# Second network of a two-block transformer: high weights meet high and low tokens in one product of 512 columns, and VectorE adds the halves of the bank

## The reference, cut to what matters

```
D_MODEL = 1024; SEQ = 256; D_FF = 4 * D_MODEL
def squared_relu_mlp(h, w1, w2):
    return jnp.square(jax.nn.relu(h @ w1)) @ w2
...
    h = modulate(rms_norm(x, norm_g[i, 2]), sh2, sc2)
    x = x + gt2 * rms_norm(squared_relu_mlp(h, mlp_w1[i], mlp_w2[i]), norm_g[i, 3])
```

## Time and profile before

| | |
|---|---|
| median of three runs | 2341.97 us (2341.75 to 2345.68) |
| the profiled execution, its own time | 2343.54 us |
| its span in the trace | 2341.7 us |
| mean granted TensorE clock | 0.975 of full speed |
| TensorE matmul / VectorE / ScalarE busy | 95% / 62% / 41% |
| `mlp_up` in the trace | from 1311.0 to 1408.4 us |
| `mlp_down` in the trace | from 1408.4 to 1505.7 us |

### The profile page before, as it was taken

One profiled execution on the slowest core, in us unless ns is written; L12 is line 12 of the kernel. 1 busy time (PEld: TensorE's weight loads), 2 busy tenths in 40 slices (PEclk: granted clock), 3 DMA queues, 4 the chain that ended last, 5 costly groups with the idle time before them and its releaser, 6 DMA issues.

```text
span 2341.7 us, 48560 instructions
## 1 busy us (share of the span) xinstructions
PE 2233.3 (95%) x21500; PEld 1848.0 (79%) x21500; DVE 1453.8 (62%) x2539; ACT 970.8 (41%) x1716; POOL 85.2 (4%) x83
## 2 busy tenths in 40 slices
PE   8999999999999999999999999998999999899998
PEld 5864488888867789999997899895677879677786
DVE  3274436867657356887763556665475877656577
ACT  2244333322323223443332563344355655544565
POOL 1000000000010000000000001020000002000000
PEclk8999999999999999999999999999999999999999
DMA  8335238656522100000002347554365853204485
GB/s 356 108 105 220 90 126 305 245 211 229 220 110 90 54 1 3 4 4 4 13 3 112 141 174 263 196 180 173 134 219 211 335 215 134 73 1 180 169 340 192
DMA packets 47745, 348.11 MB, mean 149 GB/s; under 512 B 5312, under 2 KB 5328, under 8 KB 6320
## 3 DMA queue, kind: packets, MB, share of 16 engines
q1 hardware_dynamic: 46368, 334.52, 38.2%
q0 software_dynamic: 1168, 10.50, 1.1%
HBM read 343.95 MB, written 1.05 MB: 147 GB/s over the span
## 4 chain that ended last, share of the span: by engine, by line
PE 52%; DVE 8%; ACT 3%; issue 1%; DVEq 0%; ACTq 0%
PE banks L549 10%; PE banks L2245 6%; PE banks L2257 5%; PE banks L1037 4%; PE banks L3179 3%; PE banks L3180 3%; PE banks L3181 3%; PE banks L3210 2%; PE banks L3212 2%; PE banks L3211 2%; PE banks L561 1%; PE banks L2097 1%; PE banks L2304 1%; PE banks L2279 1%; PE banks L3228 1%
## 5 line engine op out<-in xcount | busy, mean ns | idle before, releaser
L527 DVE TENSOR_TENSOR moe_w_low<-weight_slots,moe_w_high 128x2048 fp32r<-128x2048 f32 x96 | 217.9, 2288 | 61.7 <-ACT moe_w_high L518 61.0
L527 DVE TENSOR_TENSOR mlp_w_low<-weight_slots,mlp_w_high 128x2048 fp32r<-128x2048 f32 x64 | 146.5, 2288 | 157.3 <-ACT mlp_w_high L518 157.3
L518 ACT ACTIVATE mlp_w_high<-weight_slots 128x2048 fp32r<-128x2048 f32 x64 | 122.3, 1910 | 178.7 <-PE banks L549 118.9
L518 ACT ACTIVATE moe_w_high<-weight_slots 128x2048 fp32r<-128x2048 f32 x96 | 181.7, 1914 | 23.5 <-PE banks L3212 19.8
L1037 PE MATMUL banks<-arena,weight_slots 128*128 128x256 f32 (+1 forms) x512 | 141.5, 438 | 2.9 <-DVE arena L2846 1.5
L1037 PEld LDWEIGHTS banks<-arena,weight_slots 128*128 128x128 f32 x512 | 98.4, 193 | 44.3 <-issue 33.9
L3179 PE MATMUL banks<-moe_w_high,slots_x 128*128 128x512 f32 x320 | 130.3, 407 | 2.8 <-DVE moe_w_low L527 2.8
L3180 PE MATMUL banks<-moe_w_low,slots_x 128*128 128x512 f32 x320 | 126.9, 397 | 0.0
L3181 PE MATMUL banks<-moe_w_high,slots_x 128*128 128x512 f32 x320 | 126.8, 396 | 0.0
L686 DVE SCALAR_TENSOR_TENSOR arena<-weight_slots,silu_c,arena 128x256 f32<-128x256 f32 x288 | 119.0, 481 | 0.0
L2245 PE MATMUL banks<-arena 64*64 64x64 f32 (+1 forms) x1600 | 81.2, 233 | 0.0
(11 more groups left out here) (454 smaller groups left out, 5239.9 us busy)
## 6 DMA issues: line engine op xcount, KB each, us to landing
weight_slots<-weights SPq DMA_DIRECT2D x318, 1024.0 KB, 4.9
arena<-small POOLq DMA_DIRECT2D x1, 2560.0 KB, 8.9
arena<-x_t POOLq DMA_DIRECT2D x1, 2048.0 KB, 12.5
arena<-bias POOLq DMA_DIRECT2D x1, 2048.0 KB, 12.6
constants<-consts POOLq DMA_DIRECT2D x1, 1395.0 KB, 17.9
out_t<-arena SPq DMA_DIRECT2D x4, 256.0 KB, 2.3
parameters<-params POOLq DMA_DIRECT2D x1, 763.0 KB, 21.8
arena<-pool_inv POOLq DMA_DIRECT2D x1, 512.0 KB, 14.9
```

The source lines that it names most:

```text
L518: nc.scalar.activation(self.pair(j)[0], slot(j, 0, SLOT), ACT.Copy).then_inc(*act.step("high", j))
L527: nc.vector.tensor_tensor(self.pair(j)[1], slot(j, 0, SLOT), self.pair(j)[0], ALU.subtract).then_inc(*v.step("used", j))
```

## The change

In `mlp_up` (all but the first block) and in `mlp_down`, the high and low tokens of a step are read side by side by one product of 512 columns, which writes the whole bank: high weights by high tokens in columns 0 to 255, high weights by low tokens in columns 256 to 511. Low weights by high tokens then add into columns 0 to 255. For each step there are two products with two weight loads instead of three with three. The two halves of the bank are added by VectorE with a reduction over pairs (`halves_added`), which takes the place of the reader on ScalarE: in `mlp_up` ScalarE's ReLU now works in place on what VectorE wrote, in `mlp_down` its square reads `YT` and its copy of the bank is gone. VectorE's `hidden_low` for a block moves one block later in its queue. The token tiles keep their addresses and get one common name.

```diff
@@ -492,8 +492,8 @@
 
 
 
-        XHI = rounded("h_high", 0, KT, SEQ)
-        XLO = rounded("h_low", 4096, KT, SEQ)
+        X_BOTH = rounded("h_high_low", 0, 2, 2, KT, SEQ)
+        XHI, XLO = X_BOTH[:, 0, 0], X_BOTH[:, 1, 0]
 
         class Splits:
 
@@ -551,6 +551,16 @@
                                                stop=stop and n == 2 and k == tiles - 1, skip_group_check=check)
                 return ins
 
+            def columns_beside(self, pe, j, width, a, b, tiles, both, start=True, stop=True):
+
+                for k in range(tiles):
+                    nc.tensor.matmul(psum(b), self.pair(j)[0][:, k * width + a:k * width + a + P], both(k),
+                                     start=start and k == 0, stop=False)
+                for k in range(tiles):
+                    ins = nc.tensor.matmul(psum(b, 0, SEQ), self.pair(j)[1][:, k * width + a:k * width + a + P],
+                                           both(k)[:, 0], start=False, stop=stop and k == tiles - 1)
+                return ins
+
             def tokens(self, pe, j, key):
 
                 b = take_bank(pe, key)
@@ -569,6 +579,9 @@
 
         def x_low(k):
             return XLO[:, k, :]
+
+        def x_both(k):
+            return X_BOTH[:, :, 0, k, :]
 
 
         MOD = [MD[:, 96 * m:96 * m + 96].rearrange("p (t s) -> p t s", s=2) for m in range(4)]
@@ -1708,8 +1721,8 @@
             side_chains(v, block_of["wr"][0])
 
 
-        HID_HI = rounded("hidden_high", FREE, 32, SEQ)
-        HID_LO = rounded("hidden_low", FREE + 8192, 32, SEQ)
+        HID_BOTH = rounded("hidden_high_low", FREE, 2, 32, SEQ)
+        HID_HI, HID_LO = HID_BOTH[:, 0], HID_BOTH[:, 1]
         RELU, RELU2 = area(14336, 3, SEQ), area(14336 + 3 * SEQ, 3, SEQ)
         MLP = Splits("mlp", ["mlp1_1", "mlp2_1"], [(33280, 35328), (37376, 8192)])
 
@@ -1719,7 +1732,10 @@
                 j = MLP.next(pe, "mlp1_1")
                 for i in range(2):
                     b = take_bank(pe, ("x12_up", g + i))
-                    ins = MLP.columns(pe, j, 256, i * P, psum(b, 0, SEQ), KT, x_high, x_low, norm="n2_1")
+                    if g == 0:
+                        ins = MLP.columns(pe, j, 256, i * P, psum(b, 0, SEQ), KT, x_high, x_low, norm="n2_1")
+                    else:
+                        ins = MLP.columns_beside(pe, j, 256, i * P, b, KT, x_both)
                     ins.then_inc(*pe.step("x12_up", g + i))
                 pe.mark("multiplied", j)
             pe.stage("mlp_down")
@@ -1728,8 +1744,8 @@
                 for part in range(2):
                     j = MLP.next(pe, "mlp2_1")
                     pe.wait_ge(*after("hidden", "x12", 16 * part + 15))
-                    ins = MLP.columns(pe, j, P, 0, psum(b, 0, SEQ), 16, lambda k: HID_HI[:, part * 16 + k],
-                                      lambda k: HID_LO[:, part * 16 + k], start=part == 0, stop=part == 1)
+                    ins = MLP.columns_beside(pe, j, P, 0, b, 16, lambda k: HID_BOTH[:, :, part * 16 + k, :],
+                                             start=part == 0, stop=part == 1)
                     ins.then_inc(*pe.step())
                     pe.mark("multiplied", j)
                     if part == 1:
@@ -1747,10 +1763,16 @@
             for i in range(16):
                 MLP.high(act, i + MLP.ahead)
                 for f in (2 * i, 2 * i + 1):
-                    act.wait_ge(*after("x12_up", f))
-                    nc.scalar.activation(RELU[:, f % 3], psum(bank_of(("x12_up", f)), 0, SEQ), ACT.Relu).then_inc(*act.step("taken", "x12_up", f))
+                    if f < 2:
+                        act.wait_ge(*after("x12_up", f))
+                        nc.scalar.activation(RELU[:, f % 3], psum(bank_of(("x12_up", f)), 0, SEQ), ACT.Relu).then_inc(
+                            *act.step("taken", "x12_up", f))
+                        act.mark("relu", f)
+                    else:
+                        act.wait_ge(*after("taken", "x12_up", f))
+                        nc.scalar.activation(RELU[:, f % 3], RELU[:, f % 3], ACT.Relu).then_inc(*act.step("relu", f))
                 for f in (2 * i, 2 * i + 1):
-                    act.wait_ge(*after("taken", "x12_up", f))
+                    act.wait_ge(*after("relu", f))
                     if f >= 3:
                         act.wait_ge(*after("hidden", "x12", f - 3))
                     nc.scalar.activation(RELU2[:, f % 3], RELU[:, f % 3], ACT.Square).then_inc(*act.step("relu2", f))
@@ -1760,11 +1782,9 @@
             act.stage("mlp_down")
 
             def y_tile(g):
-                act.wait_ge(*after("x12_down", g))
-                src = psum(bank_of(("x12_down", g)), 0, SEQ)
-                nc.scalar.activation(squares_of("y_x12", ONE, g), src, ACT.Square).then_inc(
+                act.wait_ge(*after("taken", "x12_down", g))
+                nc.scalar.activation(squares_of("y_x12", ONE, g), YT[:, X, g, :], ACT.Square).then_inc(
                     *act.step("square", "y_x12", X, g))
-                nc.scalar.activation(YT[:, X, g, :], src, ACT.Copy).then_inc(*act.step("taken", "x12_down", g))
 
             for i in range(16):
                 MLP.high(act, 16 + i + MLP.ahead)
@@ -1777,14 +1797,33 @@
 
         def mlp_split_vector(v):
             v.stage("mlp_up")
+            def hidden_low(f):
+                v.wait_ge(*after("hidden_high", f))
+                nc.vector.tensor_tensor(HID_LO[:, f], RELU2[:, f % 3], HID_HI[:, f], ALU.subtract).then_inc(*v.step("hidden", "x12", f))
+
+            def halves_added(dst, key):
+                b = bank_of(key)
+                v.wait_ge(*after(*key))
+                nc.vector.tensor_reduce(dst, psum(b).rearrange("p (h t) -> p t h", h=2), AX.X, ALU.add).then_inc(
+                    *v.step("taken", *key))
+
             for i in range(16):
                 MLP.low(v, i + MLP.ahead)
-                for f in (2 * i, 2 * i + 1):
-                    v.wait_ge(*after("hidden_high", f))
-                    nc.vector.tensor_tensor(HID_LO[:, f], RELU2[:, f % 3], HID_HI[:, f], ALU.subtract).then_inc(*v.step("hidden", "x12", f))
+                if i:
+                    for f in (2 * i, 2 * i + 1):
+                        if f >= 3:
+                            v.wait_ge(*after("relu2", f - 3))
+                        halves_added(RELU[:, f % 3], ("x12_up", f))
+                    for f in (2 * i - 2, 2 * i - 1):
+                        hidden_low(f)
+            for f in (30, 31):
+                hidden_low(f)
             v.stage("mlp_down")
             for i in range(16):
                 MLP.low(v, 16 + i + MLP.ahead)
+                if i and i % 2 == 0:
+                    halves_added(YT[:, X, i // 2 - 1, :], ("x12_down", i // 2 - 1))
+            halves_added(YT[:, X, KT - 1, :], ("x12_down", KT - 1))
             side_chains(v, block_of["ev2_in"][0])
             EV2.low(v, 0)
```

## The result

| | before | changed |
|---|---|---|
| median of four runs | 2341.86 us | 2361.9 us (2360.2 to 2365.58) |
| the profiled execution, its own time | 2343.54 us | 2363.49 us |
| its span in the trace | 2341.7 us | 2361.7 us |

A forecast was written before the change was run, and what follows sets the result against it. The prediction took a round of VectorE and ScalarE, not TensorE, to bound changed `mlp_up`. Terms +15.1, +1.24, -3.3 and +1.0 gave +14.1 us, a median of 2356.1 us (value 2356), range 2350 to 2362.

The forecast's parts named there:

- That TensorE does not set `mlp_up`'s pace: In changed `mlp_up`, VectorE and ScalarE close a 7.00 us round without products, while TensorE needs only 5.54 us; chance 0.78.
- The round: `mlp_up`: `high`, `low`, two reductions, second ReLU, next `high` take 7.00 us instead of 5.925; 14 blocks, +15.1 us.
- The reduction's price: Each VectorE reduction over a bank's 512 numbers was taken as 0.69 us, low end 0.42, high end 0.84.
- The rival of a slow strided read: VectorE reading pairs 256 apart in the bank costs twice 0.69 us; total 2377.5 us, chance 0.05.
- The boundary: From `mlp_up` to `mlp_down`: the last ReLU starts 3.55 us after the last `low` instead of 2.31; +1.24 us.
- The end: End of `mlp_down`: last reduction and next matrix's `low` come before the reciprocal, 2.86 us after the last product; +1.0 us.
- `mlp_down`: In `mlp_down`, 15 parts each become 0.22 us shorter, with reductions hidden beside products; -3.3 us.
- The clock: Rival: TensorE's clock falls after waits, in `mlp_up` rounds (2.7 us) and at the boundary (1.65); 2360.5 us, chance 0.06.
- The sum: Whole kernel: 15.1 + 1.24 - 3.3 + 1.0 = +14.1 us, giving a median of 2356.1 us.
- The old round: Rival: reductions in `mlp_up` are hidden and its loop still goes over TensorE; +2.5 us in all, 2344.5, chance 0.03.
- It did not get faster: Rival of a faster kernel: TensorE alone sets `mlp_up`'s pace; -7.7 us in all, 2334.3, chance 0.04.
- A weight load less: Rival: saving a weight load is worth nothing, so `mlp_down` saves nothing; +17.3 us, 2359.3, chance 0.04.

The follow-up runs named there:

- late_relu: Changed kernel with ScalarE's ReLU, squares and copies of block i moved behind the rounding (`high`) of block i+2; 2339.98 us, ratio 0.9979.
- reduced_twice: Changed kernel with each reduction of `mlp_up` done twice in a row; 2384.26 us, ratio 1.0168.
- boundary_filled_3: Changed kernel with three unread products on TensorE in its wait behind the first part of `mlp_down`; 2358.93 us, ratio 1.0059.
- down_only: Kernel before with the new product and reductions in `mlp_down` alone, `mlp_up` as before; 2346.08 us, ratio 1.0.
- before_late: Kernel before with ScalarE's short work behind the next but one rounding and `hidden_low` one block later on VectorE; 2344.47 us, ratio 0.9992.
- late_relu_tuned: late_relu with VectorE's first `mod3` chain before the last two `hidden_low`, and next matrix's first `low` before the last reduction; 2341.67 us, 0.9975.

## Why the prediction was right, and where it was off

*That TensorE does not set `mlp_up`'s pace.* Right. The round was predicted at 7.00 us and is 7.01; the term of +15.1 us measured 107.34 - 92.20 = 15.1. TensorE's wait in a round shows as 1.15 us and not about 1.5: from the first product after a wait to the modelled end of the last are 5.86 us, which is more than the 5.58 between the blocks of a stream without waits (late_relu). late_relu and reduced_twice show the loop from both sides.

*The reduction's price*, 0.69 us with bounds of 0.42 and 0.84. It took 0.682, and the second of a pair is ready 0.60 after the first. The rival of a slow strided read falls.

*The boundary*, +1.24: 8.93 - 7.59 = 1.34. *The end*, +1.0: 1.00, by the mechanism named. Taking the next `low` out of the way brought 0.37 of it back.

*`mlp_down`*, -3.3: this term failed, it measured +0.16. Two things are in it. Without the clock's fall it is -2.7 (boundary_filled_3), since a wide product of this stage costs 3.65 / 16 = 0.228 us and not the 0.226 of the first network, and two parts (with one sum of a chain) follow two parts after 11.60 us and not 11.96, which is 0.18 a part and not 0.22. The rest, 2.9 us, is the fall.

*The clock.* I had it as a rival at 0.06, with 1.65 us for a fall at the boundary and 2.7 for falls in the rounds. In `mlp_up` of the changed kernel it never fell. At the boundary it fell in both traces of the changed kernel, and for some 14 products, not 8 ((6.63 - 3.76) / 0.2, from the starts of the two groups of the second part here and in boundary_filled_3; 0.2 is the 1.65 / 8 of the prediction): about 3 us. So half of this rival came true, with nearly twice its price, and its 2360.5 is nearer to the measured median than my 2356.1. The step that was mis-sized is the price of one fall, and its chance at a place where TensorE waits 2.5 us within 3.1. Both pieces of the wait stood in my working.

*The sum.* The four distances grew by 17.64 us where 14.1 was forecast, and the ratio says 17.8. The medians are 20.0 apart; the interval of the ratio reaches from 15 to 20.6 us, so the 2.4 us beyond the table may be chance. In the two profiled executions the lag grows from 17.2 us at the reciprocal to 20.0 some 130 us later, in code that is the same in both. The first step, 0.9 us, is in the products of the next matrix, where the granted clock of 10 us is 0.83 in the changed kernel (from 1535 us) and 1.00 before (from 1518 us); two more of about 1 us each come in the attention code, where the windows differ too (0.96, 0.87 and 0.66 at times after, 0.83 at others before). I did not try what brings that about. The median, 2361.9, lies 0.1 us under the top of my range. The round was right by its mechanism; that a forecast value 5.8 us too low still had the result inside its range is in part luck.

*The other rivals.* The old round did not stay, since the reductions are queued behind `low`. It did not get faster, because of the round: with it cut, it does. A weight load less is worth something: with TensorE at the pace, a block takes 5.58 us and not 5.76.

## What to carry to other kernels

Before fewer or wider products are counted as gain, look for the loop that the other engines close among themselves: follow one block from release to release over the queues, and ask which instruction stands in front of which. Replacing a reader of a bank by one on an engine that already has a long operation in that loop puts both in series; moving the short work behind the long one in the other queue cost nothing here and turned +0.8% into -0.2%. A new wait of TensorE can have a second price, the clock behind it. Where the products that follow set the pace it is paid in full (2.9 us at the boundary); where TensorE has more room than the fall takes, as in the rounds of reduced_twice, it costs nothing.

## What I had not expected

A fall of the clock is not told by the last wait alone: with 1.45 us before the second part it fell (down_only), with 1.53 us in before_late and 1.84 us in late_relu_tuned it stayed at 1.00, and with 1.15 us before each of 14 blocks, 7.01 us apart, it stayed as well. In reduced_twice it fell behind most waits of 2.6 us, but not behind one of 2.61. The time at the low level differed too: 5.50 and 5.53 us for 16 wide products in late_relu and down_only, 6.79 and 6.77 in the changed kernel, 3.8 to 3.9 at full clock.
